# Hybrid mLSTM layer with gated MLP on one core: a separate buffer for one tile's full value, GpSimd's clearing put behind it, and the last quarter of x processed in two halves with the root per token part

## What is computed

```
sh1, sc1, g1, sh2, sc2, g2 = modulation(c)          # silu(c) @ w_mod + b_mod, 2048 x 12288
hm = rms_norm(x) * (1 + sc1) + sh1
x  = x + g1 * mlstm_mixer(hm, w_in, gate_bias, h_norm, w_out)
hf = rms_norm(x) * (1 + sc2) + sh2
x  = x + g2 * conv_ffn(hf, w_up, conv_w, conv_b, w_down)
```

## Time and profile before

| | before |
|---|---|
| median of 3 runs | 1174.66 us (1174.23 to 1174.68) |
| profiled execution | 1174.24 us |
| its span | 1172.5 us |
| TensorE busy | 1154.2 us (98%) |
| VectorE busy | 920.8 us (79%) |
| ScalarE busy | 625.7 us (53%) |
| GpSimd busy | 183.1 us (16%) |
| mean granted TensorE clock | 0.998 |
| DMA, mean | 270 GB/s, 316.66 MB |

### The profile page before, as it was taken

The page is one execution under the profiler, slowest core; times in us unless marked ns, Lnnn a source line. Parts: engine busy times, 40 slices in busy tenths (PEclk is TensorE's granted clock), DMA queues, the critical chain, the costliest instruction groups (busy, mean ns, idle before and its releaser), DMA issues.

```text
span 1172.5 us, 17088 instructions
## 1 busy us (share of the span) xinstructions
PE 1154.2 (98%) x5888; PEld 980.8 (84%) x5888; DVE 920.8 (79%) x998; ACT 625.7 (53%) x911; POOL 183.1 (16%) x171
## 2 busy tenths in 40 slices
PE   5999999999999999999999999999999999999998
PEld 5888788888887888888888888888888788888887
DVE  6899897998989989888885547888885446777766
ACT  4444565665654556555554445555554445555442
POOL 0000140225320221122120001122120001221200
PEclk9999999999999999999999999999999999999999
DMA  9999999999999967988866578798775666776552
GB/s 370 397 401 402 399 365 331 370 404 390 336 402 398 397 170 221 250 226 252 233 221 245 180 232 231 210 259 234 210 235 199 213 198 185 194 194 180 194 200 72
DMA packets 260953, 316.66 MB, mean 270 GB/s; under 512 B 6328, under 2 KB 187264, under 8 KB 251944
## 3 DMA queue, kind: packets, MB, share of 16 engines
q1 hardware_dynamic: 259488, 312.50, 79.8%
q0 software_dynamic: 944, 3.34, 0.9%
q10 hardware_dynamic: 474, 0.21, 0.1%
HBM read 313.90 MB, written 2.12 MB: 270 GB/s over the span
## 4 chain that ended last, share of the span: by engine, by line
PE 96%; DMA 3%; DVE 1%; SPq 1%; ACT 0%; issue 0%; DVEq 0%
PE ps L1503 27%; PE ps L1509 14%; PE ps L1543 9%; PE ps L1545 9%; PE ps L1544 9%; PE ps L1614 7%; PE ps L1615 7%; PE ps L1617 7%; DMA m<-in_l_w_mod_dram 3%; PE ps L1622 1%; SPq L419 0%; PE ps L1649 0%; PE ps L1829 0%; PE ps L1739 0%; PE ps L1561 0%; PE ps L1559 0%
## 5 line engine op out<-in xcount | busy, mean ns | idle before, releaser
L1122 DVE TENSOR_TENSOR w_lo<-raw,w_hi 128x1024 fp32r<-128x1024 f32 x384 | 472.4, 1234 | 157.1 <-ACT w_hi L682 155.9
L682 ACT ACTIVATE w_hi<-raw 128x1024 fp32r<-128x1024 f32 x384 | 405.9, 1058 | 346.3 <-PE ps L1545 155.1
L1503 PE MATMUL ps<-hm,w_hi 128*128 128x512 f32 x1406 | 338.8, 391 | 0.2 <-DVE hm L1407 0.2
L1503 PEld LDWEIGHTS ps<-hm,w_hi 128*128 128x128 f32 x1406 | 257.3, 188 | 49.0 <-DVE hm L1407 0.4
L1509 PEld LDWEIGHTS ps<-hm,w_lo 128*128 128x128 f32 x1408 | 182.7, 191 | 8.2
L1509 PE MATMUL ps<-hm,w_lo 128*128 128x256 f32 x1408 | 185.3, 283 | 0.0
L1614 PE MATMUL ps<-w_hi,hm 128*128 128x512 f32 x380 | 150.3, 396 | 0.4 <-ACT hm L726 0.4
L1615 PE MATMUL ps<-w_lo,hm 128*128 128x512 f32 x380 | 148.2, 390 | 0.0
L1617 PE MATMUL ps<-w_hi,hm 128*128 128x512 f32 x352 | 137.3, 390 | 0.0
L1543 PE MATMUL ps<-w_hi,act_hi 128*128 128x512 f32 x344 | 134.0, 390 | 0.0
L1545 PE MATMUL ps<-w_hi,act_lo 128*128 128x512 f32 x344 | 133.9, 389 | 0.0
(11 more groups left out here) (199 smaller groups left out, 1129.0 us busy)
## 6 DMA issues: line engine op xcount, KB each, us to landing
raw<-in_l_w_up_dram SPq DMA_DIRECT2D x88, 1024.0 KB, 5.8
raw<-in_l_w_in_dram SPq DMA_DIRECT2D x96, 512.0 KB, 12.2
mod_raw<-in_l_w_mod_dram SPq DMA_DIRECT2D x48, 1024.0 KB, 8.1
raw<-in_l_w_down_dram SPq DMA_DIRECT2D x44, 1024.0 KB, 5.1
m<-in_l_w_mod_dram SPq DMA_DIRECT2D x32, 640.0 KB, 14.3
raw<-in_l_w_out_dram SPq DMA_DIRECT2D x16, 1024.0 KB, 11.3
m<-in_l_w_mod_dram SPq DMA_DIRECT2D x15, 768.0 KB, 12.9
mod_third<-in_l_w_mod_dram SPq DMA_DIRECT2D x8, 1024.0 KB, 8.1
```

The source lines that it names most:

```text
L682: nc.scalar.activation(w_hi[:, v % 4, :], raw_half(v), ACT.Copy).then_inc(w_hi_made, 1)
L1122: nc.vector.tensor_tensor(w_lo[:, v % 4, :], raw_half(v), w_hi[:, v % 4, :].bitcast(f32), ALU.subtract)\
L1503: return mm(ps[:, 4 + w % 4, :], w_hi[:, v % 4, j * P:(j + 1) * P], both, start=(k == 0), stop=stop, skip_group_check=True)
```

## The change

Four edits:
- A buffer `hm_next` for the full value of tile 6 (the seventh). VectorE makes it as soon as the shift of tiles 6 to 14 is copied, without waiting for ScalarE's high part. The copy of tile 15's shift comes behind the high parts of tiles 6 and 7.
- GpSimd's `clear_acc(3)` waits, besides, for `hm_made` 10.
- The last quarter of x is processed in three blocks: part 0 whole, part 1 in two halves, with squares, reduce, root, diagonal and spreading matmul per token part.
- The second shift is summed in four column groups of 512 (`tiled_sums`), copied by ScalarE, turned by TensorE and copied once; `wide_sums` goes.

```
@@ -66,8 +66,9 @@
     V_UP = 2 * U_UP[0]
-    SUMS_AT = (7, 11)
     FIRST_HALVES = [2 * r for r in range(4)] + [2 * r + 1 for r in range(4)]
+
+    LAST_BLOCKS = ((0, 0, QUARTER), (1, 0, SEQ), (1, SEQ, QUARTER))
@@ -146,7 +147,7 @@
         kq_rows = kq[:].rearrange("p f (t d) -> p f t d", t=TB)
-        ss_quarter = place("ss_quarter", [P, TB, 5], 192 * KB)
+        ss_quarter = place("ss_quarter", [P, TB, 6], 192 * KB)
         rstd_diag = place("rstd_diag", [P, TB, P], 193 * KB)
@@ -184,9 +185,11 @@
         first_rows = place("first_rows", [P, GROUP], tail + 2 * KB)
-        sum_rows = [first_rows, first_rows, place("sc2_rows", [P, QUARTER], 189 * KB)]
+        sum_rows = [first_rows, first_rows, place("sc2_rows", [P, QUARTER], 189 * KB),
+                    place("sh2_rows", [P, QUARTER], 189 * KB)]
         g_rows = [place("g1_rows", [P, QUARTER], 116 * KB), place("g2_rows", [P, QUARTER], 32 * KB)]
         hm_first = place("hm_first", [P, 2, SEQ], tail + 2 * KB)
+        hm_next = place("hm_next", [P, SEQ], 119 * KB)
         still = place("still", [P, 2 * P], tail + KB)
@@ -275,7 +278,7 @@
         y_scaled = sem("y_scaled")
-        x_added = sem("x_added")
+        x_added, x_part, y_part = sem("x_added"), sem("x_part"), sem("y_part")
         conv_base, tap1_made = sem("conv_base"), sem("tap1_made")
@@ -571,6 +574,7 @@
             pool.wait_ge(colsum_done, 4)
+            pool.wait_ge(hm_made, K_FIRST + 4)
             clear_acc(3)
@@ -640,12 +644,15 @@
             nc.gpsimd.memset(ss_quarter[:, :, 4], EPS).then_inc(eps_set, 1)
+            nc.gpsimd.memset(ss_quarter[:, 0, 5:6], 0.0).then_inc(eps_set, 1)
             with pool.Fori(0, 3) as i:
             clear_acc(5)
-            pool.wait_ge(ss_summed, 1)
-            nc.gpsimd.tensor_tensor(rstd, ms, minus_half, ALU.pow).then_inc(rstd_made, 1)
+            for t in range(TB):
+                pool.wait_ge(ss_summed, t + 1)
+                nc.gpsimd.tensor_tensor(rstd[:, t:t + 1], ms[:, t:t + 1], minus_half[:, t:t + 1], ALU.pow)\
+                         .then_inc(rstd_made, 1)
             for n, tiles in enumerate(CHUNKS):
@@ -762,17 +769,19 @@
                 act.wait_ge(rows_summed, s + 1)
-                nc.scalar.activation(sum_rows[s][:], ps[:, bank, 0:(GROUP, GROUP, QUARTER)[s]], ACT.Copy)\
+                nc.scalar.activation(sum_rows[s][:], ps[:, bank, 0:(GROUP, GROUP, QUARTER, QUARTER)[s]], ACT.Copy)\
                          .then_inc(rows_copied, 1)
             def later_scale_shift(n, count, bank, out, plus_one):
+                scale_shift(n, count, turned(bank, GROUP, 3),
+                            out[:, K_FIRST:KT - 1].rearrange("p (j b) -> p j b", j=3), plus_one)
+
+            def last_scale_shift(n, count, bank, out, plus_one):
                 last_tile = 2 * P + 3 * 32
                 scale_shift(n, count, ps[:, bank, last_tile:last_tile + 1], out[:, KT - 1:KT], plus_one)
-                scale_shift(n, count, turned(bank, GROUP, 3),
-                            out[:, K_FIRST:KT - 1].rearrange("p (j b) -> p j b", j=3), plus_one)
@@ -862,8 +871,9 @@
                     later_scale_shift(1, 4, 1, shift_p, False)
-                    act.wait_ge(sc_made, 6)
+                    act.wait_ge(sc_made, 5)
                     modulate_hi(0, K_FIRST, K_FIRST + 2)
+                    last_scale_shift(1, 4, 1, shift_p, False)
                 split_hi(p + 3)
@@ -872,6 +882,7 @@
                     later_scale_shift(0, 3, 2, scale_p, True)
+                    last_scale_shift(0, 3, 2, scale_p, True)
                 if p == V_PASS1 - 1:
@@ -941,6 +952,19 @@
+            def last_squares(n):
+                t, c0, c1 = LAST_BLOCKS[n]
+                if n == 1:
+                    act.wait_ge(x_part, 1)
+                else:
+                    act.wait_ge(x_added, 2 + 2 * 3 + t + 1)
+                act.wait_ge(sq_made, TB + 2 * 2 + t + 1)
+                col = 3 if n < 2 else 5
+                nc.scalar.activation(sq_junk[:, t * QUARTER + c0:t * QUARTER + c1],
+                                     x[:, t, 3 * QUARTER + c0:3 * QUARTER + c1], ACT.Square,
+                                     scale=float(D) ** -0.5, accum_out=ss_quarter[:, t, col:col + 1])\
+                         .then_inc(sq_made, 1)
+
             def squares(q, t):
@@ -964,15 +988,17 @@
                 if f == 31:
-                    squares(3, 0)
+                    last_squares(0)
                 if f < 29:
                     first_hi(f - 29)
-                if f == 32:
-                    squares(3, 1)
+                else:
+                    last_squares(1)
+                    copy_rows(3, 1)
+                    last_squares(2)
                     take_z(3)
-                    scale_shift(4, 7, ps[:, 1, 0:SUMS_AT[1]], shift_p[:, 0:SUMS_AT[1]], False)
+                    scale_shift(4, 6, turned(7, QUARTER, 4), shift_p[:].rearrange("p (j b) -> p j b", j=4), False)
                     act.wait_ge(sc_made, 8)
@@ -1003,10 +1029,8 @@
                 if k == 7:
-                    scale_shift(4, 8, ps[:, 7, 0:KT - SUMS_AT[1]], shift_p[:, SUMS_AT[1]:KT], False)
                     act.wait_ge(params_T, 3)
                     nc.scalar.activation(cvT[:], ps[:, 6, 0:4 * 2 * FT], ACT.Copy).then_inc(params_made, 1)
-                    act.wait_ge(sc_made, 9)
                     act.wait_ge(params_made, 3)
@@ -1221,12 +1245,20 @@
                 if p == V_PASS1 - 1:
-                    dve.wait_ge(sc_made, 6)
-                    modulate_lo(0, K_FIRST, K_FIRST + 2)
+                    dve.wait_ge(sc_made, 5)
+                    nc.vector.tensor_scalar(hm_next[:], xnT[:, K_FIRST, :], scale_p[:, K_FIRST:K_FIRST + 1],
+                                            shift_p[:, K_FIRST:K_FIRST + 1], ALU.mult, ALU.add)\
+                             .then_inc(hm_scaled, 1)
+                    dve.wait_ge(hm_scaled, K_FIRST + 1)
+                    dve.wait_ge(hm_hi_made, K_FIRST + 1)
+                    nc.vector.tensor_tensor(hm_lo[:, K_FIRST, :], hm_next[:], hm_hi[:, K_FIRST, :].bitcast(f32),
+                                            ALU.subtract).then_inc(hm_made, 1)
+                    modulate_lo(0, K_FIRST + 1, K_FIRST + 2)
                 split_lo(p + 3)
                 if p == V_PASS1 - 1:
+                    dve.wait_ge(sc_made, 6)
                     modulate_lo(0, K_FIRST + 2, K_FIRST + 4)
@@ -1376,24 +1408,44 @@
             last = slice(3 * QUARTER, 4 * QUARTER)
-            for t in range(TB):
-                if t == 0:
-                    dve.wait_ge(y_last, 1)
-                else:
-                    dve.wait_ge(half_done, V_OUT + 32)
-                dve.wait_ge(x_added, 2 * (3) + t + 1)
-                nc.vector.tensor_tensor(y_tmp[:, t, :], ps[:, 6 + t, :], g_bc[:, last], ALU.mult)\
-                         .then_inc(y_scaled, 1)
-                dve.wait_ge(y_scaled, 4 + 2 * (3) + t + 1)
-                nc.vector.tensor_tensor(x[:, t, last], x[:, t, last], y_tmp[:, t, :], ALU.add)\
-                         .then_inc(x_added, 1)
-            dve.wait_ge(eps_set, 1)
-            dve.wait_ge(sq_made, TB + 4 * TB)
-            nc.vector.reduce_sum(ms, ss_quarter[:], mybir.AxisListType.X).then_inc(ss_summed, 1)
-            dve.wait_ge(rstd_made, 2)
-            for t in range(TB):
+            def mean_square(t):
+                dve.wait_ge(sq_made, TB + 3 * TB + (1, 3)[t])
+                nc.vector.reduce_sum(ms[:, t:t + 1], ss_quarter[:, t, :], mybir.AxisListType.X)\
+                         .then_inc(ss_summed, 1)
+
+            def diagonal(t):
+                dve.wait_ge(rstd_made, 2 + t)
                 nc.vector.tensor_scalar(rstd_diag[:, t, :], ident[:], rstd[:, t:t + 1], None, ALU.mult)\
                          .then_inc(diag_made, 1)
+
+            def gate_block(n):
+                t, c0, c1 = LAST_BLOCKS[n]
+                cols = slice(3 * QUARTER + c0, 3 * QUARTER + c1)
+                return nc.vector.tensor_tensor(y_tmp[:, t, c0:c1], ps[:, 6 + t, c0:c1], g_bc[:, cols], ALU.mult)
+
+            def add_block(n):
+                t, c0, c1 = LAST_BLOCKS[n]
+                cols = slice(3 * QUARTER + c0, 3 * QUARTER + c1)
+                return nc.vector.tensor_tensor(x[:, t, cols], x[:, t, cols], y_tmp[:, t, c0:c1], ALU.add)
+
+            dve.wait_ge(y_last, 1)
+            dve.wait_ge(x_added, 2 * 3 + 1)
+            gate_block(0).then_inc(y_scaled, 1)
+            dve.wait_ge(y_scaled, 4 + 2 * 3 + 1)
+            add_block(0).then_inc(x_added, 1)
+            dve.wait_ge(eps_set, 2)
+            mean_square(0)
+            dve.wait_ge(half_done, V_OUT + 32)
+            dve.wait_ge(x_added, 2 * 3 + 2)
+            gate_block(1).then_inc(y_part, 1)
+            dve.wait_ge(y_part, 1)
+            add_block(1).then_inc(x_part, 1)
+            gate_block(2).then_inc(y_scaled, 1)
+            dve.wait_ge(y_scaled, 4 + 2 * 3 + 2)
+            add_block(2).then_inc(x_added, 1)
```

(50 more changed lines are left out.)

## The result

The median is 1181.74 us (six executions, 1181.56 to 1182.93) against 1174.35 before, ratio 1.0066 [1.0055, 1.0076]. Forecast: 1181.5 in 1178.0 to 1184.5, slower. The profiled execution took 1181.59 us with a span of 1179.8 (before 1172.5, +7.3). The two executions above 1182.5 were granted a mean clock of 0.994, the others 0.996 or 0.997.

What follows compares the result with a forecast made beforehand. TensorE, busy throughout 149.7 to 431.1 us, was taken as the bound, so earlier delays carry through. Profiled 1174.24 plus 5.8 (gates), 1.0 (clock), 0.1 (turn) gives 1181.1; with 0.4 for the median, 1181.5, range 1178.0 to 1184.5.

Steps and rivals of the forecast that it cites:

- The gate wait: Before the gate matmuls: the later clearing delays GpSimd's 16 operations making wg, so TensorE starts at 175.5, +5.8 us.
- Tile 6: Change from pass 0 to pass 1: own buffer and no clearing beside it shorten TensorE's waits, gain 0 to 1.2 us.
- the clearing at tile 10: Pass 1: the moved clearing may hold tile 10's scale and shift by up to 0.6 us, hidden while the gates wait.
- The clock: Around the gate matmuls: TensorE's some 6 us idle should bring a fall to half clock, +1.0 us, ends 0 and 1.7.
- half of 3.4 us, 1.7, if all of it lies on matmuls: Behind the idle time at the gates: upper end of the half-clock cost, from the earlier trace's one fall, 1.7 us.
- The turn: Out projection to up projection: later reduce +0.57, smaller root, diagonal and spread -0.49; net +0.1 us, ends -0.4 and +0.5.
- Rival 3: Out-to-up turn: without wide sums TensorE's clock falls there too, 1.6 us more, 1183.1 us in all; chance 0.23.
- The argument against this rival from the earlier trace: First transposes: 32 in 5.18 us from 17.53 left the clock at full, speaking against transposes not counting as busy.
- Rival 1: Gate columns: GpSimd's 16 operations run quickly at 0.28 us each, ending before TensorE asks; not slower, 1173.1 us; chance 0.06.
- Rival 2: Gate columns: wg_raw lands early or operations find gaps, TensorE waits only +3.1 us, little clock loss, 1177.8 us; chance 0.12.
- 0.4 for a distance of the median from the profiled execution: Whole kernel: the median of the runs taken as 0.4 us above the profiled execution, raising 1181.1 to 1181.5.

Runs made afterwards that it cites:

- experiment 1: The changed kernel without GpSimd's new wait for hm_made 10: 1174.34 us against 1174.27 for the kernel before, 1.000.
- experiment 2: The kernel before with GpSimd's new wait for hm_made 10 alone: 1181.9 us against 1174.27, 1.0067.
- experiment 7: The changed kernel with the gate columns split by four GpSimd operations of 128 elements instead of sixteen of 32: 1174.19 us against 1174.3 for the kernel before.
- experiment 3: The kernel before with hm_next and the new order of shift copies, without the later clearing, old turn: 1173.52 us against 1174.27, 0.9995.
- experiment 8: The kernel of experiment 6 with ScalarE's high parts of tiles 10 and 11 ahead of the strip copies: 1174.35 us against 1174.3 for the kernel before.
- experiment 5: The changed kernel with 24 unused fill matmuls keeping TensorE busy ahead of the wait for wg: 1179.68 us against 1174.3 for the kernel before.
- experiment 9: The kernel before with the new turn alone plus 4 fill matmuls behind the second spreading matmul: 1173.37 us against 1174.31, 0.9994.
- experiment 6: The changed kernel with the gate columns' load ahead of GpSimd's waits and their 16 operations ahead of the clearing: 1175.95 us against 1174.3 for the kernel before.

## Why the prediction was right or wrong

**The gate wait: right, for its own reason.** Forecast +5.8 with the gates at 175.5, measured +5.71 at 175.45 (+5.62 from the last matmul ahead of tile 6). Experiments 1, 2 and 7 show the cause from three sides: without the wait no slowdown, with it alone the whole of it, and with fewer operations behind it none. Inside the term two errors cancel: 13 operations, not 11, were through when VectorE fell idle, but that was at 174.51 and not at 173.9, because tile 6's gain did not reach slot 44.

**Tile 6: the low part right, the carrier of the loss wrong.** Forecast was a gain of at most 1.2 with 0.6 left by slot 44; 0.1 was left. The low part's gap closed, but by the later clearing and not by the buffer (experiments 2 and 3). I had named the clearing at tile 10 as the danger; tile 10's scale and shift took 0.41 at 152.27. It was ScalarE's order, strip copies first, that I had not laid out. Experiment 8 shows that by turning the order; it wins 0.2 there, for the next late low part stands close behind.

**The clock: mechanism right, term mis-sized.** Forecast +1.0 with an upper end of 1.7, measured +2.5 (experiment 5: 2.1 to 2.5), outside its bounds. The step that failed is "half of 3.4 us, 1.7, if all of it lies on matmuls": it took the length of the fall from the only one in the earlier trace rows. After this wait it lasted 6.83 us, 5.2 of them on matmuls. The price, half of the time at half clock that lies on matmuls, was right. In experiment 2 the clock was at half for 3.41, behind the same idle time; what decides between the two stays open.

**The turn: right within its bounds, with the wrong sign.** Forecast +0.1, measured -0.18. The reduce of part 1 came 0.41 later in the chain, not 0.57, and the root of one column takes 0.57, where I had allowed for 0.72 as an upper end; the diagonal and the spread were as counted (-0.20 and -0.22). The last squares did come behind the row copy, as foreseen. (The forecast's own sum has a slip here: a copy of 0.63 behind 433.1 ends at 433.7, not 433.6, which would have made it +0.2.)

**Rival 3** had 0.23. Its fall is not in the profiled execution of the change, and the earlier trace rows had spoken against it; but in experiments 1, 7 and 8 it is seen behind the turn, and experiment 9 prices it at 1.1 us, not 1.6. The two slower executions of the change, 1182.71 and 1182.93 at a clock of 0.994, would fit it; they have no trace, so that is argued, not shown, and one execution of experiment 3 was 1.1 us slow at a mean clock of 1.000.

The argument against this rival from the earlier trace rows does not hold as I gave it. I had read that the 32 first transposes left the clock at full. Windows of the kernel before over them:

```profile
17.50:20.50 3.00, 3.00 (x15) 3.00 (x15) 2.32 (x3) 1.33 (x3) 0.00 (x0) 1.00 1.03 399
20.60:22.70 2.10, 2.10 (x21) 2.10 (x20) 1.97 (x2) 2.06 (x5) 0.00 (x0) 1.00 1.03 399
```

The clock column shows 1.00 in both, but the trace's record of the clock begins only at 20.6, and the pace tells the rest: a transpose every 0.2 us up to there and one every 0.1 us behind it, which is also their pace in the turn before (L1829, 0.11). So they began at the lower level, and the clock rose to full while they ran. All fourteen traces show the change of pace within these transposes, between 18.8 and 25.1 us. By the Trainium skill, "TensorE: Matmul & The Clock Gate", Part 4: PE-mode transpose, the transposes of the turn would not have counted as busy; the rise in the midst of the 32 speaks against that rule in its full form, though matmuls ran right ahead of them. Whether the transposes of the turn counted is not shown.

**Rivals 1 and 2** are out: the operations took 14.7 us from 160.73 to 175.39, longer than the 11.5 before.

**Not in the forecast at all:** the 0.8 us less behind the last matmul. It cancelled half of the clock's error, so the total (+7.3 for +6.9) looks better than its terms. It is not in a wait of an engine: the last two stores are issued 0.9 and 1.3 us behind the last matmul in both kernels. It is in how the last store lands. Windows behind the bulk of it, before and then after:

```profile
1170.90:1171.65 0.75, 0.00 (x0) 0.00 (x0) 0.00 (x0) 0.00 (x0) 0.00 (x0) 0.50 0.05 11
```

```profile
1178.90:1179.80 0.90, 0.00 (x0) 0.00 (x0) 0.00 (x0) 0.00 (x0) 0.00 (x0) 1.00 0.00 0
```

Before, some 8 KB of it, packets of 1 KB one behind the other, come up to 0.75 us later than the rest; after, all packets end together. Of the fourteen traces only those of the kernel before and of experiment 2 have these late packets. Why the other kernels do not is open, and no run was made for it.

**Luck in the total.** The forecast of 1181.5 is 0.24 below the median. It contains 0.4 for a distance of the median from the profiled execution that was 0.15 in the result; this, the turn and the end behind the last matmul stand against the clock's 1.5.

## What to carry to other kernels

Before a wait is put ahead of an instruction on an in-order engine, follow everything queued behind it to its consumer and write down the slack; here it was 2.2 us, and the wait held GpSimd back by 5.3. Small operations on GpSimd that pass between VectorE's long ones cost one long operation each, so their number, not their size, is the time to reckon with. If TensorE must wait for several microseconds, give it matmuls to do, and look again for the next-latest input when one wait is taken away. Check a clock column against the pace of like matmuls, and look for a gain of under 1 us at the very end of the trace before it is credited to an edit.

## What the runs showed of the hardware that was not expected

- GpSimd's clearing of 1.8 us holds VectorE's scale and shift with one tensor input (TENSOR_SCALAR) until it ends: 0.41 became 1.00, 1.77 and 2.09 us. It does not hold the weight split with two (TENSOR_TENSOR): the one of 150.41 in the change took its usual 1.22 beside the clearing of 150.62:

```profile
150.41 1.22 DVE L1146 TENSOR_TENSOR w_lo<-raw,w_hi 128x1024 fp32r<-128x1024 f32 x1
```

- The load of the gate columns, 128 KB, issued at 122.36 where the kernel before issues it at 147.90, delayed one load of the saturated queues by 1.2 us (experiment 6).
- The same 5.55 us of idle time cost TensorE 1.5 us by the clock in one kernel and 2.5 in another; and about 2 busy us in the 3.5 ahead of the second up tile led to a fall in one execution and not in another.
- The end behind the last matmul takes 4.3 to 4.4 us (the kernel before, experiment 2) or 3.6 to 3.7 us (all others), by whether the last 8 KB of the last store land with the rest.
- TensorE's clock rose to full in the midst of the first 32 transposes, in every trace: their pace went from 0.21 to 0.11 us.
